# A first q/k tile computed while x arrives, packed narrow products, and key and pg tiles transposed by VectorE

## The reference

```python
# first block
hn = rmsnorm(h, mixer_norm)
proj = einsum('btd,de->bte', hn, w_in)
q, k, v, og, lr = split(proj, [1024, 2048, 4096, 6144])        # lr: 2 x 16 wide
gk = einsum('btzr,zrd->zbtd', lr, w_gate_up) + b_gate           # both directions
logdec = log_sigmoid(gk) / 16
o = gla(q, k, v, logdec[0]) + flip(gla(flip(q), flip(k), flip(v), flip(logdec[1])))   # 4 heads
h = h + (rmsnorm(o, out_norm) * silu(og)) @ w_out
gate_f, up = split(rmsnorm(h, ffn_norm) @ ffn_w_in, 2);  h = h + (silu(gate_f) * up) @ ffn_w_out
gate = sigmoid(rmsnorm(h, ple_norm) @ ple_w_gate)               # "pg"
x = rmsnorm(h + gate * (p @ ple_w_proj), final_norm)
# second block
q, k, v, o_g, z_a, i_pre, f_pre, u_b, z_b, g_a, g_b = partition(rmsnorm(x, norm_pre) @ w_in2)
h_t = mlstm(silu(conv(q, k)), v, i_pre + i_bias, log_sigmoid(f_pre + f_bias))         # 8 heads
y_a = sigmoid(o_g) * rmsnorm(h_t) * silu(z_a);  y_b = (pool(u_b) @ pool_w) * scale * silu(z_b)
x = x + rmsnorm((sigmoid(g_a) * (y_a @ w_a) + sigmoid(g_b) * (y_b @ w_b)) @ w_out2)
```

## Time and profile before

| | us |
|---|---|
| median of 3 runs | 2227.41 (2226.97 to 2228.48) |
| the profiled execution | 2227.32 |
| its span, first to last instruction | 2224.8 |
| TensorE busy | 2210.0 (99%) |
| VectorE busy | 1495.7 (67%) |
| ScalarE busy | 1059.6 (48%) |

### The profile page before, as it was taken

The page is one execution under the profiler, slowest core; times in us unless marked ns, Lnnn a source line. Parts: engine busy times, 40 slices in busy tenths (PEclk is TensorE's granted clock), DMA queues, the critical chain, the costliest instruction groups (busy, mean ns, idle before and its releaser), DMA issues.

```text
span 2224.8 us, 27478 instructions
## 1 busy us (share of the span) xinstructions
PE 2210.0 (99%) x10040; PEld 1829.1 (82%) x10040; DVE 1495.7 (67%) x2137; ACT 1059.6 (48%) x1321; POOL 29.1 (1%) x43
## 2 busy tenths in 40 slices
PE   8999999999999999999999999999999999999998
PEld 7888888888888888888888888888888888888887
DVE  6777697877766447777776646777455559645865
ACT  5554455544444334444455544444445555553443
POOL 0000000000000000000000100000000000000000
PEclk9999999999999999999999999999999999999999
DMA  8654466666666666666566656565755556766653
GB/s 272 178 160 117 138 218 194 195 193 197 189 196 192 194 193 190 197 189 195 183 220 191 197 151 186 172 199 171 207 177 163 170 161 192 204 191 210 196 190 114
DMA packets 282906, 413.94 MB, mean 186 GB/s; under 512 B 21055, under 2 KB 145867, under 8 KB 282283
## 3 DMA queue, kind: packets, MB, share of 16 engines
q1 hardware_dynamic: 281790, 408.55, 60.7%
q10 hardware_dynamic: 1008, 3.94, 0.5%
HBM read 410.33 MB, written 2.10 MB: 185 GB/s over the span
## 4 chain that ended last, share of the span: by engine, by line
PE 99%; DVE 0%; issue 0%; DMA 0%; ACT 0%; DVEq 0%; POOLq 0%; POOL 0%; ACTq 0%; SPq 0%
PE acc L1109 31%; PE acc L1111 31%; PE acc L1110 31%; PE mx L1248 1%; PE tp L1127 1%; PE tp L1259 1%; PE mx L1286 1%; PE mx L1281 0%; DMA H<-in_x 0%; DVE xa_lo L1991 0%; PE acc L1100 0%; PE acc L1102 0%; PE acc L1101 0%; PE mx L1093 0%; PE mx L1091 0%
## 5 line engine op out<-in xcount | busy, mean ns | idle before, releaser
L1415 DVE TENSOR_TENSOR w_lo<-raw,w_hi 128x1024 fp32r<-128x1024 f32 (+1 forms) x770 | 939.7, 1225 | 590.9 <-ACT w_hi L696 587.7
L696 ACT CAST w_hi<-raw 128x1024 fp32r<-128x1024 f32 (+1 forms) x770 | 803.1, 1046 | 935.8 <-PE acc L1111 925.9
L1109 PE MATMUL acc<-w_hi,xa_hi 128*128 128x512 f32 x2240 | 880.9, 393 | 0.0
L1111 PE MATMUL acc<-w_hi,xa_lo 128*128 128x512 f32 x2240 | 872.2, 389 | 0.0
L1110 PE MATMUL acc<-w_lo,xa_hi 128*128 128x512 f32 x2240 | 871.9, 389 | 0.0
L1111 PEld LDWEIGHTS acc<-w_hi,xa_lo 128*128 128x128 f32 x2240 | 420.5, 188 | 88.0
L1110 PEld LDWEIGHTS acc<-w_lo,xa_hi 128*128 128x128 f32 x2240 | 420.8, 188 | 85.8 <-issue 1.0
L1109 PEld LDWEIGHTS acc<-w_hi,xa_hi 128*128 128x128 f32 x2240 | 420.8, 188 | 85.9 <-issue 1.0
L1109 PE MATMUL acc<-w_hi,xb_hi 128*128 128x512 f32 x384 | 149.9, 390 | 0.2 <-DVE w_lo L1415 0.2
L1111 PE MATMUL acc<-w_hi,xb_lo 128*128 128x512 f32 x384 | 149.5, 389 | 0.0
L1110 PE MATMUL acc<-w_lo,xb_hi 128*128 128x512 f32 x384 | 149.4, 389 | 0.0
(11 more groups left out here) (263 smaller groups left out, 1166.8 us busy)
## 6 DMA issues: line engine op xcount, KB each, us to landing
raw<-in_w_in SPq DMA_DIRECT2D x192, 512.0 KB, 3.9
raw<-in_ffn_w_in SPq DMA_DIRECT2D x352, 256.0 KB, 2.9
raw<-in_gla_w_in SPq DMA_DIRECT2D x96, 512.0 KB, 3.9
raw<-in_ffn_w_out SPq DMA_DIRECT2D x88, 512.0 KB, 3.7
raw<-in_w_in SPq DMA_DIRECT2D x128, 256.0 KB, 2.9
raw<-in_gla_w_out SPq DMA_DIRECT2D x32, 512.0 KB, 4.1
raw<-in_ple_w_gate SPq DMA_DIRECT2D x32, 512.0 KB, 4.1
raw<-in_w_proj_mlstm SPq DMA_DIRECT2D x32, 512.0 KB, 3.8
```

The lines of the kernel that those rows point to most:

```text
L696: nc.scalar.copy(w_hi[:, hl, 0:kc * job.w], raw[:, slot, 0:kc * job.w]).then_inc(hi_ready, 1)
L1109: nc.tensor.matmul(a[t][:, 0:w], xh, hi, start=first, stop=False)
L1111: ins = nc.tensor.matmul(a[t][:, 0:w], xl, hi, start=False, stop=last)
L1415: nc.vector.tensor_tensor(w_lo[:, hl, 0:kc * job.w], raw[:, slot, 0:kc * job.w], w_hi[:, hl, 0:kc * job.w].bitcast(F32), ALU.subtract) \
```

## The change

**The start.** The job lr is gone. Its weights are a ninth granule of q/k tile 0 (`is_lr`). The four quarters of x are loaded between the first weight granules. TensorE turns x tiles 0 and 1 ahead of granule 0, and 2 and 3, 4 and 5, 6 and 7 right ahead of granules 1, 2 and 4 (`X_TURNED_AT`). ScalarE and VectorE work on x tile 0 ahead of their part of granule 0, tile 1 ahead of granule 1, and then two at a time ahead of granules 2, 3 and 4 (`X_AT`). 20 dummy matmuls on a zeroed corner of `stage` are put at TensorE's start (`keep_busy`), and a small copy on ScalarE. The squares of x move from granules 0 to 3 to granules 4 to 7, SP's loads of the gain vectors behind granule 1 of tile 1, and the gate pieces by one granule (`GK_AT`).

**Narrow products.** For lr and if, w_hi and w_lo of a row block stand side by side in `w_hi` (`beside`). One matmul multiplies both with x_hi, one w_hi with x_lo: two for each row block in place of three. The two halves of the result are added by a matmul with `fold`, two stacked identities, which also transposes them.

**Decay rows.** `a_split` holds the decays in fp32r, high part in rows 0 to 7, low part in rows 32 to 39, and `pick` two identities to match. One fp32r matmul replaces the fp32 one.

**Transposes.** q/k tiles 2 and 3, the keys, are turned by VectorE in eight steps hung on granules named in `KEY_TURNS`. pg tiles 0 to 2 join `BY_VECTOR`.

The diff, cut to its core:

```diff
-GK_AT = 10
+GK_AT = 11
+X_AT = {0: (0,), 1: (1,), 2: (2, 3), 3: (4, 5), 4: (6, 7)}
+X_TURNED_AT = {0: (0, 1), 1: (2, 3), 2: (4, 5), 4: (6, 7)}
...
-BY_VECTOR = {"y": 3, "wo": 3, "f2o": 3, "ya": 4, "pm": 3}
+BY_VECTOR = {"y": 3, "wo": 3, "f2o": 3, "pg": 3, "ya": 4, "pm": 3}
+Q_TILES = 2
...
-        Job("lr", 1, granules(16, 16), 2 * RANK), Job("qk", 4, full), Job("v", 4, full), Job("og", 4, full),
+        Job("qk", 1, full + granules(16, 16)), Job("qk", 3, full, first=1), Job("v", 4, full), Job("og", 4, full),
...
-        aR = at("aR", [MH, T], F32, o); o += 1024
+        a_split = at("a_split", [A_ROWS, T], F32R, o); o += 1024
+        pick = at("pick", [A_ROWS, MH], F32R, o); o += 32
...
                     a = (8 * (job.t0 + n - first - i) + j - 5 if name == "ya"
+                         else 8 * (job.t0 + n - first - i - 1) + j - 6 if name == "pg"
                          else j - 4 if job.t0 + n == first + i + 1 else -1)
...
+        KEY_TURNS = {("qk", 3, 5): (2, 0), ("qk", 3, 7): (2, 1), ("v", 0, 0): (2, 2), ("v", 0, 2): (2, 3),
+                     ("v", 1, 3): (3, 0), ("v", 1, 5): (3, 1), ("v", 1, 7): (3, 2), ("v", 2, 1): (3, 3)}
...
+        def beside(w, hl, part):
+
+            return w_hi[:, hl, 0:32 * w].rearrange("p (k two c) -> p k two c", two=2, c=w)[:, :, part, :]
...
             sp.dma_start(ident[:, :], c_ident).then_inc(loads["ident"], 16)
-            for n in range(4):
+
+            def load_x(n):
                 sp.dma_start(H[:, :, cols(n)], x[0, :, cols(n)].rearrange("(t p) d -> p t d", p=P)) \
                     .then_inc(x_landed[n], 16)
+
+            load_x(0)
...
-                if j == 7:
+                if j in (1, 2, 3):
+                    load_x(j)
+
+            def vector_loads():
                     sp.wait_ge(squared, SQ["x"] + 4)
                     sp.wait_ge(squared_too, 4)
                     sp.wait_ge(x_turned, 8)
...
+                            if (job.name, n, j) == ("qk", 1, 1):
+                                vector_loads()
...
+                if (name, n, j) == ("qk", 1, 2):
+                    act.wait_ge(consumed, 9)
+                    nc.scalar.copy(gates[0:4 * RANK, 0, 0:P], mx[0][0:4 * RANK, 0:P]).then_inc(lr_rows[0], 1)
...
+            act.wait_ge(half_set, 1)
+            nc.scalar.copy(junk[:, 0:16], half[:, :])
             act.wait_ge(gain_ready, 1)
...
-                        if job.name != "lr":
-                            split_hi(job, n, j, ns)
+                        if job is JOBS[0]:
+                            for i in X_AT.get(j, ()):
+                                x_high(i)
+                        split_hi(job, n, j, ns)
                         after_split(job, n, j, ns)
...
-                    if job.name in ("lr", "if"):
-
+                    if narrow(job, j):
+
+                        w = narrow(job, j)
+                        first, last = kk == 0, kk == kc - 1
                         xh, xl = xt_part(job, 0, k), xt_part(job, 1, k)
-                        nc.tensor.matmul(a[0][0:w, 0:T], hi, xh, start=first, stop=False)
-                        nc.tensor.matmul(a[0][0:w, 0:T], lo, xh, start=False, stop=False)
-                        ins = nc.tensor.matmul(a[0][0:w, 0:T], hi, xl, start=False, stop=last)
+                        both = w_hi[:, hl, 2 * kk * w:(2 * kk + 2) * w]
+                        if first:
+                            nc.tensor.matmul(to[0:2 * w, 0:T], both, xh, start=True, stop=False)
+                        ins = nc.tensor.matmul(to[0:w, 0:T], both[:, 0:w], xl, start=False, stop=False)
+                        if not first:
+                            ins = nc.tensor.matmul(to[0:2 * w, 0:T], both, xh, start=False, stop=last)
...
-                if made in BY_VECTOR and n < BY_VECTOR[made]:
+                if made in BY_VECTOR and n < BY_VECTOR[made] or name == "qk" and n >= Q_TILES:
                     return
...
+            def lr_folded():
+
+                for t in range(2):
+                    bank(J["lr0"].r0, t)
+                    pe.wait_ge(fold_ready, 2)
+                    pe.wait_ge(lr_rows[t], 1)
+                    nc.tensor.matmul(tp[t][:, 0:2 * RANK], gates[0:4 * RANK, t, 0:P], fold[:, 0:2 * RANK],
+                                     start=True, stop=True).then_inc(tp_ready, 1)
...
-                nc.tensor.matmul(mx[1][:, 0:T], ident[0:MH, h:h + 1].broadcast_to([MH, P]), aR[:, :],
+                nc.tensor.matmul(mx[1][:, 0:T], pick[:, h:h + 1].broadcast_to([A_ROWS, P]), a_split[:, :],
                                  start=True, stop=True)
...
+            def keep_busy(times):
+                for _ in range(times):
+                    nc.tensor.matmul(tp[0][:, 0:P], stage[:, 0, 0:P], stage[:, 0, 0:P], start=True, stop=True)
...
                     for j in range(job.G):
+                        if job is JOBS[0]:
+                            for i in X_TURNED_AT.get(j, ()):
+                                turn_x(i)
+                            if j == 0:
+                                keep_busy(10)
                         if token_halves_apart(job, n, j):
                             product(job, n, j, ns, 0)
...
+            def turn_keys(n, a):
+
+                for t in range(2):
+                    dve.wait_ge(evac[t], E(J["qk"], n))
+                own = slice(32 * a, 32 * a + 32)
+                columns = stage[own].rearrange("p t (f b c) -> p t f b c", f=4, c=32)
+                tokens = qkT[:, 4 * n:4 * n + 4, :].rearrange("p f (t a c) -> p t f a c", t=2, c=32)
+                for b in range(4):
+                    ins = nc.vector.transpose(tokens[32 * b:32 * b + 32, :, :, a, :], columns[:, :, :, b, :])
+                if a == 3:
+                    ins.then_inc(key_turned, 1)
...
+                settle(nc.vector.tensor_copy(a_split[0:MH, :], aR[:, :]))
+                nc.vector.tensor_tensor(a_split[A_LO:A_ROWS, :], aR[:, :], a_split[0:MH, :].bitcast(F32),
+                                        ALU.subtract).then_inc(a_split_ready, 1)
```

225 lines of the change are left out of this document (139 added, 86 removed), and 1 row of the table r.

## The result

The changed kernel takes 2231.07 us (median of 20 executions, 2229.34 to 2232.69), the kernel before 2227.27 in the same session (20 executions). The ratio is 1.0017, with an interval of 1.0011 to 1.0023: **slower by 3.8 us**, where 2221.0 was forecast. That is less than the 4.45 us that the prediction took for what a measurement can tell, but with 20 executions of each the interval leaves out 1. The profiled execution is the fastest of the 20: 2229.34 us, a span of 2227.4 and 1.9 around it.

What follows compares the result with a forecast made beforehand. TensorE, busy 2210.0 of 2224.8 us, was taken as the bound. Terms -2.7 (pg), -4.0 (decay rows), -1.6 (i/f), +0.4 (keys), +1.6 (start) gave -6.3: 2221.0 us, with an 8-in-10 range of 2217.5 to 2225.

Steps and rivals of the forecast that it cites:

- Start, +1.6: Kernel start: q/k begins 9.4 us earlier, but 11.0 us of transposes, waits and low-rank product come between: loses 1.6 us.
- rival (3): Start: clock falls in the 3.6 us wait, granule 4 and half of 5 at half speed: +2.7, 2223.7 us; chance 0.08.
- Keys, +0.4: Key transposes on VectorE: 1.8 us saved on TensorE, 2.2 us of waits in hosted v tiles, net +0.4 us.
- pg, -2.7: pg tiles: three rounds of transposes leave TensorE at 0.90 us each, with no wait: saves 2.7 us.
- 21.5 of 21.76 ... so no wait: pg tiles: VectorE's 14.35 busy us plus 7.1 of transposes fit the tile, as in a gb tile with 21.11 busy.
- rival (4): pg tiles: VectorE overflows, 2224 us; the pg term's bound was +3 us; chance 0.08.
- Decay rows, -4.0: mLSTM decay rows: one fp32r matmul at 0.21 us replaces 0.71, saving 0.50 a head, 4.0 us for 8 heads.
- its sign: Decay rows: the forecast is wrong if the L1356 matmuls cost more than 0.2 us.
- i/f, -1.6: Packed i/f product: 32 matmuls at 0.12 us, 3.85 instead of 5.45: saves 1.6 us; folding within 0.2 either way.
- (1): v tiles: the key steps hide because X is made earlier than thought: 2218.8 us; chance 0.17.
- (2): Start: transfers lag, each wait growing to some 2 us more: 2223 us; chance 0.10.
- Rival (5): Key transposes, output spread over four tiles, run slower; gain gone at 3.9 us a step, 2230.7 at 5 us; chance 0.04.

Runs made afterwards that it cites:

- e4: Changed kernel with both tiles of keys turned by TensorE again: 2228.39 us, a single execution.
- e5: Changed kernel with the second key tile's four VectorE steps moved to v tile 0 granules 4, 5, 6 and v tile 1 granule 2: 2228.36 us, a single execution.
- e8: Changed kernel with the array fold placed at the end of memory, so the arrays behind it stand where they stood before: 2231.06 us, a single execution.
- e6: Changed kernel with x tiles 6 and 7 turned by TensorE ahead of granule 3 instead of granule 4: 2225.56 us, a single execution.
- e9: Changed kernel without the 20 dummy matmuls at TensorE's start: 2233.75 us, a single execution.

## Why the prediction was wrong, by its own steps

The forecast was 6.3 us less than before; the profiled execution is 2.0 more, and a typical one 3.8 more.

- **Start, +1.6.** The walk held: first product 10.26 (9.95), waits 0.61 (0.9) and 3.42 (3.6), second tile 43.31 (42.75). Short were the first product (0.3), each return from transposes to products (some 0.1 us), and q/k tiles 1 and 2, which got 1.1 us longer instead of 0.9. Measured +2.3. The parts of the prediction's chain add up to 4.6 us, not 4.5; the trace has 4.46 (24.10 to 28.56).
- **The clock, rival (3), 0.08.** The step that failed is the argument from the earlier trace rows: 5.0 idle us at the end without a fall were read as proof that 3.6 would pass. In seven profiles of nine they did not. The end itself says so once more traces are there: in the 17 profiles the fall came 2.5 to 5.1 us after the last matmul, in six of them within the forecast wait of 3.6, and the kernel before is one of the two at 5.1. The rule of the Trainium skill that the prediction set beside it, "TensorE: Matmul & The Clock Gate", section "Why this matters for your kernels", was the better guide, with seven profiles for it and two against; the price here is 1.6 us. The prediction's 2.7 was half of 5.4 us, while one and a half granules at half speed would have been 4.1. One trace shows one case of something that differs from execution to execution.
- **Keys, +0.4.** Right in mechanism and place: waits of 1.6, 0.6 and 0.6 us in granules 2, 4 and 6 of v tile 1 (1.45, 0.4, 0.4). The margins between the keys' end and the scores were taken for 0.33 and 0.5 us and were worth 0.2 and 0.3. Measured -1.8 + 2.85 = +1.05. e4 and e5 show it.
- **pg, -2.7.** The step that failed, by 5.4 us, is "21.5 of 21.76 ... so no wait". It added 7.1 us to a busy sum, and the sum left out what an instruction meets. GpSimd's product costs 2.15 instead of the 0.84 that a `w_lo` pays beside it in the kernel before (2.06 instead of 1.22), and VectorE is idle for 1.47. So 21.5 + 1.3 + 1.47 = 24.3, and VectorE's pace in the trace is 24.37 us a tile. While its lead lasts the tiles still take 21.76; with the lead gone pg 3 and ub 0 take 49.9 together. The gb tile was the wrong comparison, because GpSimd does nothing in it: the earlier trace rows has 0.00 us there and 2.41 in the pg tile. That is rival (4), VectorE overflows, with 5.4 instead of 3 us; it had 0.08.
- **Decay rows, -4.0.** Measured -2.6, 0.33 a head. The term was mis-sized: entry (0.09) and exit (0.2 between L1356 and the scores) both remain, and only one of the two L1281 went, with its 0.3. The 0.21 of the prediction left the exit out. Its lower bound for the gain was 2, and its sign, an L1356 of more than 0.2 us, came true: 0.31 from start to start. No run takes this term or the next apart; both are read from the traces before and after.
- **i/f, -1.6.** Measured -1.8 in the product and +0.35 in the first qk2 tile, where the folded rows are used. The prediction put those matmuls within 0.2 either way; they cost 0.35.
- **pb, not in the sum.** +0.44, by addresses (e8).

Sum of the misses: 0.7 + 0.65 + 5.45 + 1.4 + 0.2 + 0.44, 8.8 us; 0.6 less lies outside the span. That is the 8.3 between 2221.0 and 2229.34, and the clock in the start brings the usual execution to 2231.

The range missed in two ways. Rival (4) was priced at 3 us, the bound of its term, and at the measured 5.4 it alone leads to 2226.4, above the top end of 2225. And the range held each rival by itself: (4) and, in most executions, (3) came true together, and each of the small terms erred to the same side. Rivals (1) and (2) did not come: the steps in v tile 1 cost more and not less, and with x turned earlier (e6) the weights held nothing up in the start. Rival (5) named the outcome, slower than before, but not by its cause: a step of the keys took the 1.77 us that it should. A slip without consequence: forecast, (1) and half of (2) are 0.75 and not 0.73.

## What to carry to other kernels

A busy sum close to the period proves nothing while it is made of undisturbed durations: list what the engine will stand beside and behind in the new order (here GpSimd's product and a cast behind `xa_hi`), and add those waits before comparing. An instruction that moves its input from a PSUM bank to SBUF may change what it contends with; look for the GpSimd instruction that overlaps it. When work is moved to a less busy engine, place each piece in a gap that the trace shows (VectorE's 3.61 and 2.36 us here), and the same transposes that cost 2.85 us cost nothing. A wait like the 3.4 us of this start should be priced with a fall of the clock behind it (1.6 us here), whatever a single trace shows.

## What the runs showed of the hardware

- A VectorE instruction with two SBUF inputs and GpSimd's product of 1024 columns hold each other up: 0.48 became 2.63 us for `xa_lo`, and GpSimd's 2.40 became 3.30 when a `w_lo` was first. VectorE's transposes, with one input, lasted 0.44 us each with the product and without it.
- The clock fell at 3.4 us of idle time in seven profiles of nine, and behind 1.8 us in pg or ub 0 in five of nine. At the end of the kernels it fell 2.5 to 5.1 us after the last matmul. Each fall within a kernel lasted 3.41 us. In pg 3, where VectorE set the pace, it cost nothing; in the start it cost 1.6 us, in ub 0 of e9 0.85.
- With 8 transposes as TensorE's first work of any length (e9) the clock came up at 13.99 us, with the kernel before's 32 at 10.90, with the dummy matmuls ahead of them at 4.7 to 7.7.
- With all arrays behind a new one of 192 bytes moved, the matmuls that take their 128x128 operand from `yb_hi` became slower (232 and 229 instead of 227 ns), and moving the arrays back undid that.
